# Moving the key rotation, the second values and the compressed scores one stage earlier in a hybrid-block kernel

## What is computed

```python
y_ssm = _mamba2_mixer(...) @ w_ssm_out
y_nsa = _nsa_mixer(...) @ w_nsa_out
merged = sigmoid(hn @ w_gs) * y_ssm + sigmoid(hn @ w_ga) * y_nsa
# inside _nsa_mixer
q, kc, ksl, kw = (_rope(t, cos, sin) for t in (q, kc, ksl, kw))
kcmp = silu(windows(kc) @ cmp_w1_k) @ cmp_w2_k     # 31 windows of 32 keys per group, likewise vcmp
pc = masked_softmax(q @ kcmp * scale)              # compressed scores; o_cmp = pc @ vcmp
sel = top_k(pc @ overlap + prio)                   # four selected blocks of 64 keys
out = g0 * o_cmp + g1 * selected_attention + g2 * window_attention
```

## Time and profile before

| | us |
|---|---|
| median of three runs (2874.52 to 2879.25) | 2876.37 |
| the profiled execution, whole | 2872.95 |
| its span in the trace | 2871.1 |
| PE busy in the span | 2658.9 (93%) |
| DVE busy | 1531.3 (53%) |
| ACT busy | 983.9 (34%) |
| `ssm_out`, from its first ACT instruction | 1995.8 to 2152.6 |
| `nsa_project`, from PE's first matmul | 2152.8 to 2204.2 |
| `nsa_compress` | 2204.2 to 2238.8 |
| `nsa_compressed` | 2238.8 to 2283.7 |
| `nsa_attention` | 2283.7 to about 2456 |

### The profile page before, as it was taken

How to read it: one execution, slowest core, us unless ns; L and a number is a source line. 1 busy time by engine, 2 the same in 40 slices (tenths; PEclk the granted TensorE clock), 3 DMA queues, 4 the chain that set the end, 5 groups by cost and what they waited for, 6 DMA issues and landing times. The chain is left out here.

```text
span 2871.1 us, 34800 instructions
## 1 busy us (share of the span) xinstructions
PE 2658.9 (93%) x14191; PEld 2100.6 (73%) x14191; DVE 1531.3 (53%) x2178; ACT 983.9 (34%) x1363; POOL 335.7 (12%) x193
## 2 busy tenths in 40 slices
PE   6999999999999999999998989999988698998984
PEld 5977788888787778888886887887766565775542
DVE  4473555544536545645565644655736588455313
ACT  3254632222323554322232322333521288420001
POOL 0000004432300000323440000001000000011100
PEclk8899999999989999999999989999998799888997
DMA  4211134444312112442442232243324100248996
GB/s 134 74 59 59 59 100 136 133 147 132 95 59 74 59 59 74 132 141 94 146 133 74 88 89 90 95 89 110 120 83 161 59 31 2 76 187 358 418 419 244
DMA packets 274792, 351.27 MB, mean 122 GB/s; under 512 B 55108, under 2 KB 251972, under 8 KB 261956
## 3 DMA queue, kind: packets, MB, share of 16 engines
q1 hardware_dynamic: 266084, 327.97, 34.0%
q0 software_dynamic: 8448, 20.98, 2.0%
q10 hardware_dynamic: 96, 0.02, 0.0%
HBM read 332.13 MB, written 25.17 MB: 124 GB/s over the span
## 5 line engine op out<-in xcount | busy, mean ns | idle before, releaser
L199 PE MATMUL ps<-h_hi,w_hi 128*128 128x512 f32 x1760 | 706.1, 401 | 33.8 <-PEq L2091 8.0
L200 PE MATMUL ps<-h_lo,w_hi 128*128 128x512 f32 x1760 | 692.0, 393 | 0.0
L201 PE MATMUL ps<-h_hi,w_lo 128*128 128x512 f32 x1760 | 691.9, 393 | 0.0
L176 ACT ACTIVATE w_hi<-w_raw 128x2048 fp32r<-128x2048 f32 (+1 forms) x170 | 322.3, 1896 | 812.6 <-PE ps L201 804.4
L181 DVE TENSOR_TENSOR w_lo<-w_raw,w_hi 128x2048 fp32r<-128x2048 f32 (+1 forms) x170 | 431.1, 2536 | 302.1 <-ACT w_hi L176 302.1
L199 PEld LDWEIGHTS ps<-h_hi,w_hi 128*128 128x128 f32 x1760 | 335.0, 190 | 115.3 <-issue 47.0
L201 PEld LDWEIGHTS ps<-h_hi,w_lo 128*128 128x128 f32 x1760 | 334.3, 190 | 71.5
L200 PEld LDWEIGHTS ps<-h_lo,w_hi 128*128 128x128 f32 x1760 | 335.1, 190 | 69.8 <-issue 2.9
L201 PE MATMUL ps<-merged_hi,w_lo 128*128 128x512 f32 x640 | 252.8, 395 | 0.0
L199 PE MATMUL ps<-merged_hi,w_hi 128*128 128x512 f32 x640 | 252.8, 395 | 0.0
L200 PE MATMUL ps<-merged_lo,w_hi 128*128 128x512 f32 x640 | 252.8, 395 | 0.0
(11 more groups left out here) (471 smaller groups left out, 3806.1 us busy)
## 6 DMA issues: line engine op xcount, KB each, us to landing
w_raw<-in_w_in SPq DMA_DIRECT2D x284, 256.0 KB, 3.6
w_raw<-in_w_up SPq DMA_DIRECT2D x128, 256.0 KB, 3.5
w_raw<-in_w_down SPq DMA_DIRECT2D x128, 256.0 KB, 3.6
room<-in_w_ada SPq DMA_DIRECT2D x96, 256.0 KB, 6.0
expert_over_h<-in_w_exp_down SPq DMA_DIRECT2D x10, 1024.0 KB, 25.9
w_raw<-in_w_out SPq DMA_DIRECT2D x32, 256.0 KB, 3.6
spilled<-projected POOLq DMA_DIRECT2D x32, 256.0 KB, 2.4
w_raw<-in_w_ssm_out SPq DMA_DIRECT2D x32, 256.0 KB, 3.6
```

Source lines behind the costliest of these rows:

```text
L176: act.activation(self.hi[:, q, :, 0:cols], raw[:, q, :, 0:cols], ACT.Copy).then_inc(self.hi_ready, 1)
L199: pe.matmul(out, w[0], x[0], start=start, stop=False)
L200: pe.matmul(out, w[0], x[1], start=False, stop=False)
L201: return pe.matmul(out, w[1], x[0], start=False, stop=stop)
```

## The change

Nothing that is computed changes. The work is moved:

1. In `ssm_out` at s = 3 the second values are written pair by pair, each as soon as `out(3)` has read the pair that lay there (new semaphore `y_used`).
2. The positions, the six key chunks (kc, ksl, kw) and the eight query chunks are loaded by SP in `ssm_out`, behind the last SSMO tiles; `angles` runs on DVE at s = 5, the sines on ACT at s = 5, and the six key chunks are rotated there (PE after `out(5)` and `out(6)`, DVE at s = 6 and s = 7).
3. `nsa_project` rotates only the eight query chunks, two before each gate chunk, and takes over the window additions of `nsa_compress` and the load of `cmp_w1_k`.
4. The compressed scores move from `nsa_compressed` to the end of `nsa_compress`; `nsa_compressed` puts its second gate chunk behind both `turn`s.
5. The split of the last tile of a stage moves into the next one: (GA, 1) to the start of `nsa_project`, (NSAO - 1, 1) to the start of `nsa_compress`, (NSAO, 1) to `nsa_attention`, its high part at the start on ACT and its low part at step 32 of 64 on DVE. SP's loads follow: (GA + 1, 1) and (NSAO, 0) in `nsa_project`, (NSAO, 1) in `nsa_compress`.

Buffers change place with it: the SSM's arrays are given back before `ssm_out`, and sines, cosines and rotation scratch lie in the gate array.

```diff
@@ ssm_out
             @block.sync
             def _(sp):
-                self.issue2(sp, P_GS, P_GA)
+                for m in range(P_GS + 2, P_GA):
+                    pair(m)
+                sp.wait_ge(normed, 8)
+                sp.dma_start(pos, self.d["positions_2"].to_broadcast([P, S])).then_inc(angle, 16)
+                sp.wait_ge(low, 8)
+                for i in range(6):
+                    sp.dma_start(self.rp[:, 8 + i, :], self.spilled(self.key_chunk(i))).then_inc(k_landed[i], 16)
+                for c in range(8):
+                    sp.dma_start(self.rp[:, c, :], self.spilled(16 + c)).then_inc(q_landed, 16)
+                pair(P_GA)
+                W.issue(sp, B2 + P_GA + 1, 0, self.tile2(P_GA + 1, 0))
+                sp.wait_ge(q_landed, 16 * 8)
...
+                        if s == 3 and k % n == n - 1 and k < KC - 1:
+                            mm.then_inc(y_used, 1)
...
                 for s in range(1, 8):
                     out(s)
+                    if s == 5:
+                        rotate(0)
+                        rotate(1)
+                    if s == 6:
+                        for i in range(2, 6):
+                            rotate(i)
...
-                    if s == 4:
+                    if s == 3:
+                        for p in range(4, 7):
+                            act.wait_ge(y_used, p - 3)
+                            high(p)
                         W.done(act, SO + 1, 1)
-                        for p in range(4, 8):
-                            high(p)
-                    W.split_hi(act, m + 1, q)
+                        high(7)
+                    if s == 5:
+                        act.wait_ge(folded, 2)
+                        for i in range(2):
+                            act.activation(self.trig[:, i], ang[:, i], ACT.Sin).then_inc(sines, 1)
+                    if s < 7:
+                        W.split_hi(act, m + 1, q)
...
-                    if s == 4:
+                    if s == 3:
                         for p in range(4, 8):
                             low_of(p)
+                    if s == 5:
+                        angles(dve)
+                    for i in {6: (0, 1), 7: (2, 3, 4, 5)}.get(s, ()):
+                        rope(i)
                     if s >= 4:
...
-                    W.split_lo(dve, m + 1, q)
+                    if s < 7:
+                        W.split_lo(dve, m + 1, q)
@@ nsa_project
                     for c in range(n):
+                        i = 2 * (2 * t + c)
+                        rotate(i)
+                        rotate(i + 1)
                         gate_chunk(pe, W, (GA, t), c, self.pst[:, t, c], self.h)
-                        for i in range((0, 0, 6, 8)[2 * t + c]):
-                            rotate(at)
-                            at += 1
...
-                angles(dve)
-                dve.wait_ge(sines, 2)
+                rope(0)
+                rope(1)
+                W.split_lo(dve, GA, 1)
+                windows(self.rp[:, 8:10, :], self.blk_k, "pek")
+                for i in range(2, 4):
+                    rope(i)
                 W.split_lo(dve, GA + 1, 0)
-                for i in range(6):
+                for i in range(4, 8):
                     rope(i)
-                W.split_lo(dve, GA + 1, 1)
-                for i in range(6, 14):
-                    rope(i)
+                dve.wait_ge(done, 8)
+                dve.wait_ge(v_landed, 16 * (NG + 4))
+                windows(self.vc, self.blk_v, "pev")
@@ nsa_compress
-                W.split_lo(dve, tile[0] + 1, tile[1])
+                W.split_lo(dve, tile[0], 1)
                 dve.wait_ge(kv_ready, 1)
                 dve.tensor_copy(self.kcmp[:], self.ps[:, 4, 0:NB]).then_inc(taken, 1)
...
+                W.split_lo(dve, tile[0] + 1, tile[1])
...
+                pe.wait_ge(taken, 1)
+                for g in range(NG):
+                    for b in range(TB):
+                        for r in range(HPG):
+                            h = HPG * g + r
+                            rows = slice(HD * (h % 2), HD * (h % 2) + HD)
+                            pe.matmul(self.cmp_scores(g, r % 2)[:, b, r // 2], self.rp[rows, h // 2, b * P:(b + 1) * P],
+                                      self.kcmp[rows, g * NC:(g + 1) * NC], start=True, stop=True)
...
                 act.activation(self.dtgn[:, :, SSM_HEADS:], self.dtgn[:, :, SSM_HEADS:], ACT.Sigmoid).then_inc(gated, 1)
+                W.split_hi(act, tile[0], 1)
@@ nsa_compressed
-                scores(0)
-                scores(1)
                 W.ready(pe, *tile)
                 gate_chunk(pe, W, tile, 0, self.ps[:, 6, :], self.h)
-                gate_chunk(pe, W, tile, 1, self.ps[:, 7, :], self.h)
                 turn(0)
                 turn(1)
+                gate_chunk(pe, W, tile, 1, self.ps[:, 7, :], self.h)
...
-                take_gate(act, W, tile, self.ps[:, 6:8, :], self.gate[:, 3 * n:4 * n, :])
                 take(0)
                 take(1)
+                W.done(act, *tile)
+                act.activation(self.gate[:, 3 * n:4 * n, :], self.ps[:, 6:8, :], ACT.Copy).then_inc(W.evicted[tile[1]], 1)
...
                 second(0)
-                W.split_lo(dve, tile[0] + 1, tile[1])
                 second(1)
@@ nsa_attention
                 for n in range(len(steps)):
+                    if n == len(steps) // 2:
+                        self.W.split_lo(dve, B2 + P_NSAO, 1)
                     evict(n)
...
+                self.W.split_hi(act, B2 + P_NSAO, 1)
                 exps(0)
```

More of the change, by code:

```diff
@@ L1875, in ssm_out @@
                 "opened", "gated", "squared", "added", "summed", "mean", "root", "inverse", "normed", "rounded", "low", "sig"))
+            angle, steps, folded, sines, turned, cosd, sind, done, q_landed = (sem(x) for x in (
+                "angle", "steps", "folded", "sines", "turned", "cosd", "sind", "done", "q_landed"))
+            y_used, k_landed = sem("y_used"), [sem(f"k_landed{i}") for i in range(6)]
             landed = self.z_landed
-            sb = lambda nm, s, dt=F32: st.enter_context(nc.sbuf_tensor(nm, s, dt))
-            z, acc = sb("silu_z", [P, 2, n, S]), sb("ssm_squares", [P, 2, n, S])
+            z, acc = self.z, self.acc
+            pos, ang, turns = acc[:, 1, 0].bitcast(I32), self.trig, self.rope_a
+            tc, ts = self.rope_a, self.gate[:, 0:2, :]
             y_hi, y_lo = self.parts(st, "yn", KC)
@@ L1884, in ssm_out, with angles, pair @@
             PAIRS_Y, GROUPS = 8, SSM_G
+            def angles(dve):
+                link = Link(dve, steps)
+                dve.wait_ge(angle, 16)
+                link(dve.tensor_copy(ang[:, 0], pos[:]))
+                link(dve.tensor_scalar(ang[:, 0], ang[:, 0], self.c("inv"), None, ALU.mult))
+                link(dve.tensor_scalar(turns[:, 0], ang[:, 0], 1.0 / TWO_PI, ROUND, ALU.mult, ALU.add))
+                link(dve.tensor_scalar(turns[:, 0], turns[:, 0], ROUND, None, ALU.subtract))
+                for part in (PI_A, PI_B, PI_C):
+                    link(dve.scalar_tensor_tensor(ang[:, 0], turns[:, 0], -part, ang[:, 0], ALU.mult, ALU.add))
+                link(dve.tensor_scalar(ang[:, 1], ang[:, 0], float(np.pi / 2), None, ALU.add))
+                link(dve.tensor_scalar(turns[:, 1], ang[:, 1], float(np.pi), -TWO_PI, ALU.is_gt, ALU.mult))
+                link(dve.tensor_tensor(ang[:, 1], ang[:, 1], turns[:, 1], ALU.add))
+                edge = 3.1415925
+                for i in range(2):
+                    dve.tensor_scalar(ang[:, i], ang[:, i], edge, -edge, ALU.min, ALU.max).then_inc(folded, 1)
             @block.sync
             def _(sp):
-                self.issue2(sp, P_GS, P_GA)
+                def pair(m):
+                    for q in range(2):
+                        W.issue(sp, B2 + m, q, self.tile2(m, q))
+                for m in range(P_GS + 2, P_GA):
[10 more added lines that the diff above has]
+                sp.wait_ge(q_landed, 16 * 8)
             @block.gpsimd
@@ L2099, in nsa_project @@
-            tc, ts = sb("rope_cos", [P, 2, S]), sb("rope_sin", [P, 2, S])
+            turned, cosd, sind, done, v_landed = (sem(x) for x in ("turned", "cosd", "sind", "done", "v_landed"))
+            ts = st.enter_context(nc.sbuf_tensor("rope_sin", [P, 2, S], F32))
+            tc = self.rope_a
             block = st.enter_context(nc.Block())
-            order = (8, 9, 10, 11, 12, 13, 0, 1, 2, 3, 4, 5, 6, 7)
             rot_ps = lambda i: self.ps[:, (2, 3, 6, 7)[i % 4], :]
-            kept = {16 + c: self.rp[:, c, :] for c in range(8)}
@@ L2121, in _ @@
+                for x in range(4):
+                    part = slice(4 * x, 4 * x + 4)
+                    sp.dma_start(self.w1[:, part], self.d["cmp_w1_k_2"][0].rearrange("(k p) n -> p k n", p=P)[:, part]).then_inc(v_landed, 16)
+                W.issue(sp, B2 + P_GA + 1, 1, self.tile2(P_GA + 1, 1))
+                W.issue(sp, B2 + P_NSAO, 0, self.tile2(P_NSAO, 0))
```

(11 more changed lines are left out.)

150 lines of the change are left out of this document (72 added, 78 removed).

## The result

| | before | after |
|---|---|---|
| median of the runs, us | 2876.42 (2874.52 to 2879.25) | 2840.47 (2837.23 to 2843.20) |
| the profiled execution, us | 2872.95 | 2837.23 |
| its span | 2871.1 | 2835.4 |
| PE busy in the span | 2658.9 | 2648.3 (93%) |
| `nsa_project`, from PE's first matmul | 2152.8 | 2145.1 |

The ratio of after to before is 0.9877, 95% interval [0.9865, 0.9889]: 1.2% or 36 us faster. The spans differ by 35.7 us.

The account below looks back on a forecast made before the run. PE, busy 93%, loses time to five stalls and the slow clock behind them. Attention starts 36.3 us earlier, less 1.0 lost there: 35.3 us, 2837.6 for the profiled execution, 2841 for the median, put at 2840; range 2831 to 2851.

Parts of the forecast that it names:

- The order of the stages and who is late: Stage starts forecast: `nsa_project` 2145.1, `nsa_compress` 2177.5, `nsa_compressed` 2215.7, `nsa_attention` 2247.4; last engines: DVE, PE, PE, then ACT's gate copy.
- The stalls: Five PE waits before the change: 5.6 us in `ssm_out`; 6.9, 8.0, 5.4 at stage ends; 9.8 in `nsa_compressed`.
- The second values: In `ssm_out`, rounding pairs during `out(3)` removes `out(4)`'s 5.6 us wait and its slow clock: 7.9 us.
- `nsa_project`: DVE again ends the stage last, after 31.9 instead of about 51 us; next stage begins 32.4 us after this one.
- The first chunk of the compression: At the start of `nsa_compress`, PE begins at clock 0.50 after 3.2 us idle: 8.0 us, 5.3 of them slow.
- a start at full clock a plain gain of 2.6: Range term: `nsa_compress` begun at full clock saves 2.6 us; weights' first quarter free at 9.9, SP's tile issued by 7.8.
- The scores: At the end of `nsa_compress`: 8.7 us, between 6.9 if the clock holds and 13.9 if it falls at once.
- run fast for some 5 us: Scores start behind dense chunks in `nsa_compress`, so full clock lasts some 5 us, slow after; gives the 8.7 us.
- The split ahead of the copy: At the end of `nsa_compress`, a `kcmp` copy waiting for the weight split, as before, would have cost 2.3 us.
- `nsa_compressed`: DVE's chain takes 27.3 us; PE's last gate chunk, 8.0 at slow clock, ends later; stage 31.7 against 45.0 us.
- the hole: In `nsa_attention`, DVE's 2.3 us low split at step 32 delays PE: taken as 2.0 us, between 0 and 2.3.
- Rival (c): Hole at attention's step 32 drops the clock, PE slow for a third of remaining 70 us: about 10 us, 2850; chance 0.05.

Follow-up runs that it names:

- chunk first: The changed kernel with the gate's chunk 1 in `nsa_compressed` ahead of both turns instead of behind them: 2838.39 us, ratio to before 0.9863 [0.9845, 0.9882].
- chunk between: The changed kernel with the gate's chunk 1 in `nsa_compressed` between the two turns instead of behind both: 2839.19 us, ratio to before 0.9877 [0.9862, 0.9892].

## Why the prediction was right

**The order of the stages and who is late** came out as put. `nsa_project` begins at 2145.15 (2145.1 forecast) after 1.8 us of idle at clock 1.00; `nsa_compress` at 2177.46 (2177.5), behind the value windows on DVE; `nsa_compressed` at 2217.0 (2215.7); the attention at 2248.0 (2247.4), behind PE's last chunk; and the attention with what follows gives back little. The gain at the attention's start is 35.7 us by the trace against 36.3 forecast, and the total 35.7 against 35.3.

**The stalls** that the prediction starts from are five; two more of the earlier trace rows's stretch, 5.2 and 4.3 us, are passed over. The sum is not hurt, because both lie inside stages whose lengths were taken as they were. But the 5.2 us are the slow start of the attention that came back with the chunk first.

**The second values**: forecast 7.9, measured 7.8 to 8.4 in the two runs that take the part out or make it alone.

**`nsa_project`**, the largest share, was forecast at 32.4 us and takes 32.3; it is read from the trace alone.

**The first chunk of the compression** took 7.2 us, not 8.0: the clock still held for its first 0.9 us. By itself this put the scores at 2205.8 instead of 2206.7. It is luck: behind the same 3.4 us of idle the chunk took 7.2 us in six of the twelve profiles, 8.2 to 8.3 in four and 5.6 in two. And the step that calls a start at full clock a plain gain of 2.6 has the DMA wrong: it lets the first quarter be free at 9.9 us, behind SP's tile at 7.8, but at full clock it is free at about 7.5, and then PE waits.

**The scores** are the term that was mis-sized: 8.7 forecast, 10.9 measured, inside its ends of 6.9 and 13.9. The step that failed is "run fast for some 5 us": they ran fast for 3.3, and for 3.3 to 4.7 in eight more traces, which have them between 9.6 and 10.9 where nothing delayed them, 13.9 behind a 4.1 us wait, and none at the 6.9. The two speeds, 53 and 103 ns, are as put. By the rule of the Trainium skill, page "TensorE: Matmul & The Clock Gate", section "LDWEIGHTS (loading the stationary operand)", that was weighed there, the scores would have kept to 107 ns at either clock; 60 of them in 3.2 us at 0.98 show that they don't. If two of them share one load, as the prediction reads the row, the rule would give 53 ns at either clock, and then it is the 103 ns at 0.50 that doesn't agree.

**The split ahead of the copy** was passed over at 2.3 us. It is 7: 4.1 of waiting, because the split waits for ACT, and 3.0 because the idle time costs the scores their fast part. The step counted the split's own length and neither what it waits for nor the clock. It was on the side of the gain and in both stages' lengths already, so the sum didn't suffer.

**`nsa_compressed`**: 31.0 against 31.7. DVE's chain was 27.2 (27.3), and PE's last chunk, 7.7 instead of 8.0, was late by 3.4. Chunk first and chunk between took exactly this away.

**The attention**: the hole was put at 2.0 between 0 and 2.3, and is 1.6, or 2.5 with the clock's fall; the start gained about as forecast. To the next stage's first matmul the attention is 173.9 us against 172.8, 1.1 more, where 1.0 was forecast. Rival (c) had its trigger, for the clock did fall behind the hole in this profile, but for 3.4 us, not for a third of 70. Of eight profiles with this hole the clock fell in three, each time for 3.4 us, and held in five: a loss of 0.9 us, not of 10.

What follows the attention was 1.1 us shorter in this profile than in that of before, with stretches of lower clock at other places. That is not the change's work, and together with the attention's 1.1 and the 0.6 missing at its start it closes the sum. So that the total came within 0.4 us of the forecast is in part luck.

## What to carry to other kernels

A move of thin matmuls across a stage end is worth the tail of other engines that they cover, not their length: put them where DVE still has copies and splits to do, and put their operand's copy ahead of any split that waits for another engine. When a chain on DVE paces a stage, look at what TensorE is left to do behind the last thing that DVE gave it; but idle time moved from inside a stage to its end can be paid again as a slow start of the next. Price a hole of 2 us by a stretch between two like instructions within one trace, since medians whose intervals are 7 us wide and more won't show it. Before you count a stage's faster start as a gain, look for the DMA that was just in time for the slow one.

## What the runs showed of the hardware

- Scores with 64 rows and 31 columns lost full clock 3.3 us after they began (3.3 to 4.7 in nine profiles), though TensorE was never idle; with three 512-column products after every sixteen of them it stayed at 1.00 for all 15.2 us, in one profile. Changing between the two shapes cost about 0.36 us for each pair of changes.
- A DVE operation on 128x2 values took 2.63 us instead of 0.16 while GpSimd's 4.51 us subtraction ran, and ended with it. The operations on DVE that read PSUM in the same time kept their length (0.69 us), and so did a reciprocal of 128x2 with one operand in SBUF (0.16). The Trainium skill, page "Trainium Architecture — The Big Picture", section "What this means for kernel authors", says that DVE and GpSimd share a pair of ports, held by one of them at a time. By that rule, the trace agrees.
- A stall of 1.2 to 1.8 us did not have one price. At 2143.4 in after and in all its sisters the clock held; behind the DMA wait of 1.2 and 1.7 us it fell for 13.7 and 17.1 us, and behind the hole of 1.8 us in the attention it fell for 3.4 us in three profiles and held in five. Behind 3.4 us of idle at the start of the compression stage the first 24 matmuls took 5.6, 7.2 or 8.2 us, by the execution. What TensorE did before and after differs between these places, and no run holds it fixed.
